# Attention on pairs of heads: alternating row halves and column halves of the array

## The chip, the cores and the metric

The kernel runs on one core of one Trainium2 chip. The metric is the device time of one execution in microseconds (us). "The span" is the time from the first to the last instruction of the profiled execution. The engines are named as the profile names them: PE is TensorE (matmuls and transposes), PEld its weight loads, DVE is VectorE, ACT is ScalarE, POOL is GpSimd, SP issues the DMAs.

## The reference

The program is one decoder block on 256 tokens and 1024 features: two attention branches, gated and mixed, and then a layer of 16384 experts. What matters here is the attention, 8 heads of 64 features in both branches, over two blocks of 128 query tokens. `o_cmp` attends to 15 compressed tokens; with 256 tokens all four selection blocks are chosen, and the window of 512 covers everything, so `o_sel` and `o_win` are plain causal attention with different keys and values.

```python
def block_fn(bidx):
    ...
    sc = jnp.einsum('bghtd,bgcd->bghtc', qb, kc) * scale
    pc = jax.nn.softmax(jnp.where(cmask, sc, NEG), axis=-1) * has_c
    o_cmp = jnp.einsum('bghtc,bgcd->bghtd', pc, vc)
    ...
    ps = jax.nn.softmax(jnp.where(smask[:, :, None], ss, NEG), axis=(-2, -1))
    o_sel = jnp.einsum('bghtnl,bgtnld->bghtd', ps, vs_g)
    ...
    pw = jax.nn.softmax(jnp.where(wmask, sw, NEG), axis=-1)
    o_win = jnp.einsum('bghtk,bgkd->bghtd', pw, vwb)
    o_nsa = gb[0] * o_cmp + gb[1] * o_sel + gb[2] * o_win
    z = jnp.einsum('bhtd,bhsd->bhts', qsb, k_sb) * scale
    m = pos[None, :] < t[:, None]
    l1m = jnp.where(m, jax.nn.log_sigmoid(-z), 0.0)
    after = lax.cumsum(l1m, axis=3, reverse=True) - l1m
    a_w = jnp.where(m, jnp.exp(jax.nn.log_sigmoid(z) + after), 0.0)
    o_sb = jnp.einsum('bhts,bhsd->bhtd', a_w, v_sb)
```

## The kernel before

The order of every engine is written out by hand, and semaphores tie the engines together. Everything up to the experts is a stream of 78 weight tiles of 128x1024 floats. SP loads tile n into `raw[n % 4]`; ACT copies it to `hi[n % 3]` in the reduced type fp32r (`split_hi(n)`, L749), DVE writes the rest to `lo[n % 3]` (`split_lo(n)`, L1094), and PE multiplies by both. So `split_hi(n)` must wait until PE has used tile n-3. A tile of the gates (`gate_tile(g)`, tile `T_GATE + g`, g from 0 to 15) is 24 matmuls of 128x256 into PSUM bank `g % 2`; ACT reads it with `gate_exp(g)` (L870).

The eight heads lie between the last tile of `vsb` (L344 to L346) and the mixing of the branches (`branch(0)`, first line L575). In the loop over heads `hh` PE does, in this order:

- `gate_tile(2 * hh)`;
- six transposes of the probabilities of this head (L519) and two of its compressed ones (L523); called T below;
- `scores(hh + 1)`: the score products of the next head (L471, L472, L474); called S;
- the sums of logs of the stick branch, with triangular and all-ones weights (L531 to L533); called L;
- `gate_tile(2 * hh + 1)`;
- `sticks(hh + 1)`: the stick products (L486, L487);
- the value products (L546 to L548 for the first branch, L553 and L554 for the stick branch); called V.

All these products are in f32, and PE executes each as two instructions, so a row of the profile with x2 is one product. The scores and sticks contract over the 64 features of a head. Those of an even head lie on partitions 0 to 63 and those of an odd head on 64 to 127, so only half of the array's rows takes part. The value products give 64 output partitions, 0 to 63 for an even head and 64 to 127 for an odd one, so only half of its columns takes part.

```python
r0, a, g = 64 * (hh % 2), hh // 2, hh // 4
r = slice(r0, r0 + HD)
```

Around PE the chain of a head is this. The softmax: DVE adds the mask (L1268, L1269) and takes maxima (L1274 to L1277), ACT exponentiates in six pieces with their sums (`exps`, L879), DVE normalises (L1292 to L1296), PE transposes, ACT copies the transposes out (L903). The sticks: ACT takes Abs, Exp and Ln (`softplus`, L864 to L866), DVE makes two arrays from it (`stick_logs`, L1284, L1285), POOL masks one (L1575), PE sums, DVE adds (`x_ready`, L1314), ACT exponentiates (L907), POOL masks again (L1580), PE multiplies by the values, ACT copies both results out (`osb_out`, L887). Before the loop ACT copies the stick values out of banks 2 and 1 (`vsb_out`, L894, L895).

Of the kernel before, what the change touches and what calls it, by code (L numbers as in the profile page):

```python
# [30 lines left out]
P = 128  # L31
# [57 lines left out]
def build(nc, x_d, wpre_d, u_d, v_d, par_d, cst_d, kep_d, out_d):  # L89
    with ExitStack() as ctx:  # L90
# [66 lines left out]
        gcc, gsc = carve(64), carve(64)  # L157
        nrm_n, nrm_a, nrm_b, nrm_q, nrm_c = carve(512), carve(512), carve(512), carve(512), carve(128)
# [16 lines left out]
        sm = carve(2 * 828).rearrange("p (q c) -> p q c", q=2)  # L175
        att = carve(2 * 32).rearrange("p (q c) -> p q c", q=2)
        pT = carve(1024)
        sbt = carve(5 * 384).rearrange("p (k c) -> p k c", k=5)
# [136 lines left out]
        def _(pe):  # L315
# [145 lines left out]
            def scores(hh):  # L461
                r0, a, g = 64 * (hh % 2), hh // 2, hh // 4
                r = slice(r0, r0 + HD)
                if hh == 0:
                    pe.wait_ge(S("qkT_out"), 4)
                    pe.wait_ge(S("kcT_out"), 1)
                else:
                    pe.wait_ge(S("masked"), hh)
                for br, o in ((0, bank[4]), (1, bank[5])):
                    k = kT[r, 2 * br + g, :]  # L470
                    pe.matmul(o[:, 0:P], qT[r, a, 0:P], k[:, 0:P], start=True, stop=True)  # L471
                    m = pe.matmul(o[:, P:384], qT[r, a, P:T], k[:, 0:T], start=True, stop=True)  # L472
                for b in range(TB):
                    m = pe.matmul(bank[4][:, 384 + NC_ * b:384 + NC_ * (b + 1)], qT[r, a, b * P:(b + 1) * P],  # L474
                                  kcT[r, g, 0:NC_], start=True, stop=True)
                m.then_inc(S("scores"), 1)

            def sticks(hh):
                r0, a = 64 * (hh % 2), hh // 2
                r = slice(r0, r0 + HD)  # L480
                if hh == 0:
                    pe.wait_ge(S("qksb_out"), 4)
                    pe.wait_ge(S("vsb_out"), 1)
                else:
                    pe.wait_ge(S("x_ready"), hh)
                pe.matmul(bank[2][:, 0:T], ksbT[r, a, 0:P], qsbT[r, a, :], start=True, stop=True)  # L486
                m = pe.matmul(bank[2][:, T:384], ksbT[r, a, P:T], qsbT[r, a, P:T], start=True, stop=True)  # L487
# [12 lines left out]
            for i in range(4):  # L500
                normal(T_VSB + i, i, [bank[2][:, :], bank[1][:, :]])
                if i == 0:
                    scores(0)
            sticks(0)
            for hh in range(NH):
                r0, a, g = 64 * (hh % 2), hh // 2, hh // 4
                gate_tile(2 * hh)

                pe.wait_ge(S("probs"), hh + 1)
                if hh == 0:  # L510
                    pe.wait_ge(S("qksb_out"), 4)
                else:
                    pe.wait_ge(S("pT_out"), 2 * hh)
                    pe.wait_ge(S("cmpT_out"), hh)
                    pe.wait_ge(S("osb_out"), hh)
                q = hh % 2
                for br in range(2):
                    for c in range(3):
                        m = pe.transpose(bank[6 + br][:, c * P:(c + 1) * P],  # L519
                                         sm[:, q, 414 * br + c * P:414 * br + (c + 1) * P], ident)  # L520
                m.then_inc(S("pT"), 1)
                for b in range(TB):
                    m = pe.transpose(bank[3][0:NC_, b * P:(b + 1) * P],  # L523
                                     sm[:, q, 384 + NC_ * b:384 + NC_ * (b + 1)], ident)
                m.then_inc(S("cmpT"), 1)
                if hh + 1 < NH:
                    scores(hh + 1)

                pe.wait_ge(S("l_masked"), hh + 1)
                L = sbt[:, 1, :]  # L530
                pe.matmul(bank[2][:, 0:T], cv_("tri"), L[:, 0:T], start=True, stop=False)  # L531
                pe.matmul(bank[2][:, P:T], cv_("ones"), L[:, T:384], start=False, stop=True)
                m = pe.matmul(bank[2][:, T:384], cv_("tri"), L[:, T:384], start=True, stop=True)  # L533
                m.then_inc(S("after"), 1)
                if hh + 1 < NH:
                    gate_tile(2 * hh + 1)
                    sticks(hh + 1)

                pe.wait_ge(S("pT_out"), 2 * hh + 2)
                pe.wait_ge(S("cmpT_out"), hh + 1)  # L540
                o = bank[3][r0:r0 + HD, 0:T]
                for br in range(2):
                    vcol = slice((2 * br + g) * HD, (2 * br + g + 1) * HD)
                    p0 = 384 * br

                    pe.matmul(o, vsw[:, 0, vcol], pT[:, p0:p0 + T], start=(br == 0), stop=False)  # L546
                    pe.matmul(o[:, P:T], vsw[:, 1, vcol], pT[:, p0 + T:p0 + 384], start=False, stop=False)
                m = pe.matmul(o, vcs[0:NC_, g * HD:(g + 1) * HD], pT[0:NC_, 768:1024], start=False, stop=True)  # L548
                m.then_inc(S("onsa"), 1)
                pe.wait_ge(S("a_ready"), hh + 1)  # L550
                o = bank[3][r0:r0 + HD, T:2 * T]
                vcol = slice(hh * HD, (hh + 1) * HD)
                pe.matmul(o, vsb[:, 0, vcol], sbt[:, 4, 0:T], start=True, stop=False)  # L553
                m = pe.matmul(o[:, P:T], vsb[:, 1, vcol], sbt[:, 4, T:384], start=False, stop=True)  # L554
                m.then_inc(S("osb"), 1)

# [179 lines left out]
        def _(act):  # L736
# [121 lines left out]
            def softplus(hh):  # L858

                act.wait_ge(S("z_ready"), hh + 1)  # L860
                if hh:
                    act.wait_ge(S("z_read"), hh)
                sp_ = sbt[:, 2, :]
                link(act.activation(sp_, bank[2][:, 0:384], ACT.Abs))  # L864
                link(act.activation(sp_, sp_, ACT.Exp, scale=-1.0))
                act.activation(sp_, sp_, ACT.Ln, bias=1.0).then_inc(S("softplus"), 1)  # L866

            def gate_exp(g):
                act.wait_ge(tile_used, T_GATE + g + 1)
                act.activation(gates[:, g, :], bank[g % 2][:, 0:T], ACT.Exp,  # L870
                               scale=-1.0).then_inc(S("gate_exp"), 1)

            def exps(hh):

                q = hh % 2
                act.wait_ge(S("negmax"), hh + 1)
                for c, (c0, w_) in enumerate(((0, P), (P, T), (414, P), (414 + P, T), (384, NC_), (384 + NC_, NC_))):
                    x_ = sm[:, q, c0:c0 + w_]
                    m = act.activation(x_, x_, ACT.Exp, bias=att[:, q, 6 + c:7 + c], scale=SCALE,  # L879
                                       accum_out=att[:, q, 12 + c:13 + c])  # L880
                m.then_inc(S("exped"), 1)

            def osb_out(hh):

                r0, a = 64 * (hh % 2), hh // 2
                act.wait_ge(S("osb"), hh + 1)
                act.activation(oT.rearrange("p (k a) t -> p k a t", k=2)[r0:r0 + HD, :, a, :],  # L887
                               bank[3][r0:r0 + HD, :].rearrange("p (k t) -> p k t", k=2), ACT.Copy).then_inc(S("osb_out"), 1)

            exps(0)  # L890
            split_hi(31)
            split_hi(32)
# [3 lines left out]
            softplus(0)  # L896
            for hh in range(NH):
                split_hi(T_GATE + 2 * hh + 3)
                act.wait_ge(S("pT"), hh + 1)
                if hh:  # L900
                    act.wait_ge(S("onsa"), hh)
                for br in range(2):
                    act.activation(pT[:, 384 * br:384 * (br + 1)], bank[6 + br][:, 0:384],  # L903
                                   ACT.Copy).then_inc(S("pT_out"), 1)
                gate_exp(2 * hh)
                act.wait_ge(S("x_ready"), hh + 1)
                act.activation(sbt[:, 0, :], sbt[:, 0, :], ACT.Exp).then_inc(S("x_exp"), 1)  # L907
                if hh + 1 < NH:
                    exps(hh + 1)
                    osb_out(hh)  # L910
                    softplus(hh + 1)
# [861 lines left out]
```

## Time and profile before

| what | value |
|---|---|
| time, median of 3 runs (lowest to highest) | 1107.07 us (1105.69 to 1108.93) |
| the profiled execution: its time | 1109.66 us |
| the profiled execution: its span, mean granted clock | 1107.9 us, 0.995 |
| PE busy | 1081.7 us, 98% of the span |
| DVE busy | 876.1 us, 79% |
| ACT busy | 695.8 us, 63% |
| the heads: end of the first `vsb` tile to the start of `branch(0)` | 92.95 to 216.87 us |

A busy PE is not a full PE: matmuls are pipelined, so the time that one costs in a sequence is the distance from its start to the start of the next, not its own duration.

### The profile page before, as it was taken

What the parts mean: (1) busy time and instruction counts of PE and PEld (TensorE: products, weight loads), DVE (VectorE), ACT (ScalarE), POOL (GpSimd) and SP (SyncE); (2) the same over time, 40 slices, a digit from 0 to 9 for tenths busy, and PEclk for the clock granted to TensorE, in tenths of its full rate; (3) what the DMA queues carried; (4) which work ended last, traced back from release to release, by engine and by line L of the source; (5) the groups of instructions that cost most, each with busy time, mean ns of one, the idle gap of its engine ahead of it and who ended that gap; (6) DMA issues with size and microseconds to landing.
All of it is one profiled execution on the core that took longest, in us unless ns stands there. A gap on an engine that the chain in (4) does not pass through costs nothing.

```text
span 1107.9 us, 22321 instructions
## 1 busy us (share of the span) xinstructions
PE 1081.7 (98%) x7162; PEld 979.0 (88%) x7162; DVE 876.1 (79%) x1702; ACT 695.8 (63%) x1246; POOL 331.8 (30%) x286
## 2 busy tenths in 40 slices
PE   6999999999999999999999999999999999999998
PEld 5788888798999999999999999978888888888887
DVE  5754666577999998988999999999999996444444
ACT  4345665566444444447777777799999996554443
POOL 0000122100700111662333333224444444445553
PEclk9999999899999999999999999999999999999999
DMA  7464122255545556554444444444444455555553
GB/s 258 148 234 153 58 77 78 75 189 162 202 135 178 183 171 199 180 184 145 166 151 163 159 153 164 158 152 165 160 169 162 160 175 204 190 195 195 196 190 114
DMA packets 50017, 181.34 MB, mean 164 GB/s; under 512 B 5552, under 2 KB 5680, under 8 KB 49968
## 3 DMA queue, kind: packets, MB, share of 16 engines
q1 hardware_dynamic: 49968, 180.72, 48.3%
q8 instruction: 27, 0.44, 0.2%
q14 instruction: 22, 0.18, 0.1%
HBM read 178.60 MB, written 2.10 MB: 163 GB/s over the span
## 4 chain that ended last, share of the span: by engine, by line
PE 89%; DVE 7%; ACT 2%; DMA 1%; issue 1%; POOL 0%; SPq 0%; ACTq 0%; POOLq 0%; DVEq 0%
PE bank L713 32%; PE bank L658 10%; PE bank L659 9%; PE bank L660 9%; PE bank L672 5%; PE bank L330 4%; PE bank L331 4%; PE bank L332 3%; DVE lo L1376 2%; PE bank L599 2%; DMA raw<-wpre_d 1%; PE bank L344 1%; PE bank L345 1%; PE bank L346 1%; PE bank L546 1%; PE bank L408 1%
## 5 line engine op out<-in xcount | busy, mean ns | idle before, releaser
L970 ACT ACTIVATE hi<-raw 128x1024 fp32r<-128x1024 f32 x253 | 268.2, 1061 | 245.8 <-PE bank L660 151.3
L1376 DVE TENSOR_TENSOR lo<-raw,hi 128x1024 fp32r<-128x1024 f32 x253 | 315.3, 1251 | 104.7 <-ACT hi L970 103.9
L658 PE MATMUL bank<-xhi,hi 128*128 128x256 f32 x1024 | 293.6, 287 | 0.8 <-DVE lo L1376 0.8
L659 PE MATMUL bank<-xlo,hi 128*128 128x256 f32 x1024 | 289.5, 283 | 0.0
L660 PE MATMUL bank<-xhi,lo 128*128 128x256 f32 x1024 | 289.4, 283 | 0.0
L1635 POOL TENSOR_TENSOR auxl<-big,auxh 128x256 fp32r<-128x256 f32 x126 | 168.9, 1341 | 200.2 <-ACT auxh L1006 200.2
L658 PEld LDWEIGHTS bank<-xhi,hi 128*128 128x128 f32 x1024 | 196.0, 191 | 2.2 <-issue 1.2
L659 PEld LDWEIGHTS bank<-xlo,hi 128*128 128x128 f32 x1024 | 196.3, 192 | 0.0
L660 PEld LDWEIGHTS bank<-xhi,lo 128*128 128x128 f32 x1024 | 196.0, 191 | 0.0
L713 PE MATMUL bank<-hi,auxh 128*128 128x512 f32 x508 | 161.2, 399 | 0.5 <-POOL auxl L1635 0.3
L713 PE MATMUL bank<-lo,auxh 128*128 128x512 f32 x508 | 157.2, 391 | 0.0
L713 PE MATMUL bank<-hi,auxl 128*128 128x512 f32 x508 | 156.8, 390 | 0.0
L1094 DVE TENSOR_TENSOR lo<-raw,hi 128x1024 fp32r<-128x1024 f32 x73 | 96.5, 1331 | 43.5 <-ACT hi L749 43.1
L749 ACT ACTIVATE hi<-raw 128x1024 fp32r<-128x1024 f32 x73 | 76.9, 1056 | 63.2 <-PE bank L332 39.6
L713 PEld LDWEIGHTS bank<-lo,auxh 128*128 128x128 f32 x508 | 95.3, 188 | 21.1
L713 PEld LDWEIGHTS bank<-hi,auxl 128*128 128x128 f32 x508 | 95.4, 188 | 20.7
L1622 POOL TENSOR_TENSOR oneB<-kep,eT 128x512 fp32r<-128x512 f32 x64 | 66.9, 1047 | 150.3 <-PE bank L672 140.5
L713 PEld LDWEIGHTS bank<-hi,auxh 128*128 128x128 f32 x508 | 90.6, 189 | 16.6 <-POOL auxl L1635 0.8
L1506 DVE TENSOR_REDUCE gsum<-bank 128x256 f32<-128x512 f32 x128 | 87.6, 685 | 7.7 <-PE bank L672 1.5
L1497 DVE TENSOR_TENSOR oneA<-same,gw 128x512 fp32r<-128x512 f32 x128 | 87.2, 681 | 0.0
L1000 ACT ACTIVATE oneB<-oneB 128x512 fp32r<-128x512 f32 x128 | 80.1, 626 | 2.1
L993 ACT ACTIVATE oneB<-kep,eT 128x128 fp32r<-128x128 f32 x256 | 81.0, 388 | 0.0
(270 smaller groups left out, 1773.6 us busy)
## 6 DMA issues: line engine op xcount, KB each, us to landing
raw<-u_d SPq DMA_DIRECT2D x128, 512.0 KB, 3.3
raw<-v_d SPq DMA_DIRECT2D x128, 512.0 KB, 3.2
raw<-wpre_d SPq DMA_DIRECT2D x78, 512.0 KB, 4.0
big<-x_d SPq DMA_DIRECT2D x2, 512.0 KB, 3.7
out_d<-big SPq DMA_DIRECT2D x2, 512.0 KB, 5.5
big<-out_d SPq DMA_DIRECT2D x2, 512.0 KB, 5.1
out_d<-big SPq DMA_DIRECT2D x4, 256.0 KB, 2.1
big<-cst_d SPq DMA_DIRECT2D x1, 719.5 KB, 8.1
```

The lines of the kernel that those rows point to most:

```text
L658: pe.matmul(out, wh, xhi[:, k, :], start=(k == 0), stop=False)
L659: pe.matmul(out, wh, xlo[:, k, :], start=False, stop=False)
L660: m = pe.matmul(out, wl, xhi[:, k, :], start=False, stop=(k == KT - 1))
L713: m = pe.matmul(bank[2 * b + f][:, :], a_, w_[:, s, f * 512:(f + 1) * 512], start=(first and st_ == 0), stop=False, skip_group_check=True)
L970: act.activation(hi[:, n % SPLIT, :], raw[:, n % RING, :], ACT.Copy).then_inc(hi_done, 1)
L993: m = act.activation(oneB[:, g % 2, t, :], iota, ACT.Square, bias=i2, scale=-1.0)
L1000: act.activation(oneB[:, g % 2, :, :], oneB[:, g % 2, :, :].bitcast(F32), ACT.Relu, bias=1.0, scale=-1.0).then_inc(S("oneB_ready"), 1)
L1094: dve.tensor_tensor(lo[:, n % SPLIT, :], raw[:, n % RING, :], hi[:, n % SPLIT, :].bitcast(F32), ALU.subtract).then_inc(lo_done, 1)
L1376: dve.tensor_tensor(lo[:, n % SPLIT, :], raw[:, n % RING, :], hi[:, n % SPLIT, :].bitcast(F32), ALU.subtract).then_inc(lo_done, 1)
L1497: dve.tensor_tensor(oneA[:, g % 2, :, :, :], eq_, w_.unsqueeze(3).broadcast_to([P, 4, 2, HALF]), ALU.mult).then_inc(S("oneA_ready"), 1)
L1506: dve.tensor_reduce(gsum[:, :, :], parts, AXX, ALU.add).then_inc(S("bank67_read"), 1)
L1635: pool.tensor_tensor(auxl[:, s * T:(s + 1) * T], big[:, bass.ds(i * (UNROLL * T) + b * T, T)], auxh[:, s * T:(s + 1) * T].bitcast(F32), AL ...
```

## The change

Four pairs `p` take the place of eight heads. Within `scores`, `sticks` and the value products the calls of the two heads of a pair stand in turn: one on the lower half of the rows (or columns), the next on the upper half. The score products of the two heads go to banks 4 and 5, the sticks to banks 2 and 1, both value results to bank 3 on the two halves of its partitions. The gate tiles lose bank 1 and all use bank 0, so each waits for the `gate_exp` of the one before. ACT, DVE and POOL do the same work on the same elements; what can be done for two heads in one instruction is (Exp, Ln, the maxima, the masks of the sticks, the copy of the results). The scores come in two steps per pair, one per branch, each waiting for DVE to have read the one before.

```diff
+            rows = (slice(0, HD), slice(HD, P))
+            def scores(p, br):
...
+                    pe.wait_ge(S("masked"), 2 * p + br)
+                for c0, q_, w_ in ((0, slice(0, P), P), (P, slice(P, T), T)):
+                    for i, r in enumerate(rows):
+                        m = pe.matmul(bank[4 + i][:, c0:c0 + w_], qT[r, p, q_], kT[r, 2 * br + g, 0:w_],
+                                      start=True, stop=True)
+                if br == 0:
+                    for b in range(TB):
+                        for i, r in enumerate(rows):
+                            m = pe.matmul(bank[4 + i][:, 384 + NC_ * b:384 + NC_ * (b + 1)], qT[r, p, b * P:(b + 1) * P],
+                                          kcT[r, g, 0:NC_], start=True, stop=True)
...
             def gate_tile(g):
-                if g >= 2:
-                    pe.wait_ge(S("gate_exp"), g - 1)
+                if g:
+                    pe.wait_ge(S("gate_exp"), g)
                 else:
-                    pe.wait_ge(S("vsb_out"), 2)
-                tposed(T_GATE + g, bank[g % 2][:, 0:T])
+                    pe.wait_ge(S("kcT_out"), 1)
+                tposed(T_GATE + g, bank[0][:, 0:T])
...
+                for br in range(2):
+                    vcol = slice((2 * br + g) * HD, (2 * br + g + 1) * HD)
+                    p0 = 384 * br
+                    for i, r in enumerate(rows):
+                        pe.matmul(bank[3][r, 0:T], vsw[:, 0, vcol], pT[i][:, p0:p0 + T], start=(br == 0), stop=False)
+                    for i, r in enumerate(rows):
+                        pe.matmul(bank[3][r, P:T], vsw[:, 1, vcol], pT[i][:, p0 + T:p0 + 384], start=False, stop=False)
...
+            for p in range(4):
+                gate_tile(4 * p)
+                if p == 0:
+                    sticks(0)
+                probs_T(p, 0)
+                gate_tile(4 * p + 1)
+                probs_T(p, 1)
+                if p < 3:
+                    scores(p + 1, 0)
+                if p:
+                    log_sums(p)
+                gate_tile(4 * p + 2)
+                if p == 0:
+                    log_sums(p)
+                if p < 3:
+                    scores(p + 1, 1)
+                    sticks(p + 1)
+                    gate_tile(4 * p + 3)
+                by_values(p)
             gate_tile(2 * NH - 1)
...
+            for p in range(4):
+                gate_exp(4 * p)
+                if p == 0:
+                    softplus(0)
+                pT_out(p, 0)
+                split_hi(T_GATE + 4 * p + 3)
+                gate_exp(4 * p + 1)
+                split_hi(T_GATE + 4 * p + 4)
+                pT_out(p, 1)
+                act.wait_ge(S("x_ready"), p + 1)
+                act.activation(stick_x, stick_x, ACT.Exp).then_inc(S("x_exp"), 1)
+                gate_exp(4 * p + 2)
+                split_hi(T_GATE + 4 * p + 5)
+                if p < 3:
+                    softplus(p + 1)
+                    gate_exp(4 * p + 3)
+                    exps(p + 1, 0)
+                    osb_out(p)
+                    exps(p + 1, 1)
+                    split_hi(T_GATE + 4 * p + 6)
+            osb_out(3)
...
+            for p in range(4):
+                split_lo(T_GATE + 4 * p + 3)
+                split_lo(T_GATE + 4 * p + 4)
...
+                split_lo(T_GATE + 4 * p + 5)
+                if p < 3:
+                    mask_scores(p + 1, 1)
+                    maxima(p + 1)
+                    stick_logs(p + 1)
+                    normalise(p + 1, 0)
+                    normalise(p + 1, 1)
+                    split_lo(T_GATE + 4 * p + 6)
```

The first place is PE's scores and sums of logs, inside the loop. Before, one head's scores are followed by its sums (L471 to L474 are the scores, L531 to L533 the sums):

```order
L471 MATMUL bank<-big 128x128
L472 MATMUL bank<-big 128x256
L471 MATMUL bank<-big 128x128
L472 MATMUL bank<-big 128x256
L474 MATMUL bank<-big 128x15 x2
L531 MATMUL bank<-big 128x256
L532 MATMUL bank<-big 128x128
L533 MATMUL bank<-big 128x128
```

In the change the four calls of a row such as `128x256 x2` or `128x15 x4` belong to both heads in turn, and the first branch's scores of a pair stand ahead of the sums of the pair before, the second branch's behind the next gate tile:

```order
L479 MATMUL bank<-big 128x128 x2
L479 MATMUL bank<-big 128x256 x2
L484 MATMUL bank<-big 128x15 x4
L532 MATMUL bank<-big 128x256
L533 MATMUL bank<-big 128x128
L534 MATMUL bank<-big 128x128
L532 MATMUL bank<-big 128x256
L533 MATMUL bank<-big 128x128
L534 MATMUL bank<-big 128x128
```

What moved: the same products for two heads stand together, in one run for the first branch and one for the second, instead of in one run for each head.

The second place is PE's value products. Before, for one head (L546 to L548 into partitions of the first branch's result, L553 and L554 for the sticks):

```order
L546 MATMUL bank<-big 64x256
L547 MATMUL bank<-big 64x128
L546 MATMUL bank<-big 64x256
L547 MATMUL bank<-big 64x128
L548 MATMUL bank<-big 64x256
L553 MATMUL bank<-big 64x256
L554 MATMUL bank<-big 64x128
```

In the change, for a pair:

```order
L546 MATMUL bank<-big 64x256 x2
L548 MATMUL bank<-big 64x128 x2
L546 MATMUL bank<-big 64x256 x2
L548 MATMUL bank<-big 64x128 x2
L550 MATMUL bank<-big 64x256 x2
L556 MATMUL bank<-big 64x256 x2
L559 MATMUL bank<-big 64x128 x2
```

Each call now has its twin on the other column half right behind it.

The third place is ACT at the end of an iteration. Before (L879 is `exps`, L887 `osb_out`, L864 to L866 `softplus`, L749 `split_hi`, L870 `gate_exp`):

```order
L879 ACTIVATE big<-big 128x15 x2
L887 ACTIVATE big<-bank 64x2x256
L864 ACTIVATE big<-bank 128x384
L865 ACTIVATE big<-big 128x384
L866 ACTIVATE big<-big 128x384
L749 ACTIVATE hi<-raw 128x1024
L870 ACTIVATE big<-bank 128x256
```

In the change (L909 is `exps`, L925 `osb_out`, L780 `split_hi`, L901 `gate_exp`):

```order
L909 ACTIVATE big<-big 128x256
L909 ACTIVATE big<-big 128x15 x2
L925 ACTIVATE big<-bank 128x2x256
L909 ACTIVATE big<-big 128x128
L909 ACTIVATE big<-big 128x256
L909 ACTIVATE big<-big 128x128
L909 ACTIVATE big<-big 128x256
L909 ACTIVATE big<-big 128x15 x2
L780 ACTIVATE hi<-raw 128x1024
L901 ACTIVATE big<-bank 128x256
```

Two runs of `exps` with `osb_out` between them and one `split_hi` now stand ahead of the `gate_exp` that the second gate tile of the next pair waits for.

## Rows read from the trace of the kernel before

**Rows 1.** The page: busy time by engine; the group of `split_lo`.

```profile
PE 1081.7 (98%) x7162; PEld 979.0 (88%) x7162; DVE 876.1 (79%) x1702; ACT 695.8 (63%) x1246; POOL 331.8 (30%) x286
...
L1094 DVE TENSOR_TENSOR lo<-raw,hi 128x1024 fp32r<-128x1024 f32 x73 | 96.5, 1331 | 43.5 <-ACT hi L749 43.1
```

**Rows 2.** Stretches: length, busy time of PE, PEld, DVE, ACT, POOL, granted clock.

```profile
208.00:217.00 9.00, 9.00 (x40) 6.52 (x41) 1.52 (x2) 2.18 (x3) 0.99 (x1) 0.62 0.20 72
...
123.70:137.10 13.40, 13.40 (x94) 11.44 (x93) 8.65 (x21) 8.04 (x24) 2.95 (x2) 1.00 0.25 80
```

**Rows 3.** PE in time: start, duration, line, shape (weights' rows*columns, moving operand).

```profile
110.30 0.82 PE L519 MATMUL bank<-kep,big 128*128 128x128 f32 x6
...
111.27 0.49 PE L471 MATMUL bank<-big 64*128 64x128 f32 x2
111.59 0.59 PE L472 MATMUL bank<-big 64*128 64x256 f32 x2
112.03 0.38 PE L471 MATMUL bank<-big 64*128 64x128 f32 x2
...
112.68 0.51 PE L474 MATMUL bank<-big 64*128 64x15 f32 x4
113.12 0.70 PE L531 MATMUL bank<-big 128*128 128x256 f32 x2
...
114.03 0.36 PE L330 MATMUL bank<-xhi,hi 128*128 128x256 f32 x1
...
117.06 0.70 PE L486 MATMUL bank<-big 64*128 64x256 f32 x2
...
117.91 0.65 PE L546 MATMUL bank<-big 128*64 128x256 f32 x2
118.39 0.38 PE L547 MATMUL bank<-big 128*64 128x128 f32 x2
118.61 0.60 PE L546 MATMUL bank<-big 128*64 128x256 f32 x2
...
120.73 0.38 PE L330 MATMUL bank<-xhi,hi 128*128 128x256 f32 x1
```

**Rows 4.** PE in time where it waits: before the loop and in its last head.

```profile
105.05 0.67 PE L486 MATMUL bank<-big 64*128 64x256 f32 x2 [1.78 <-ACT big L894]
...
206.48 0.70 PE L531 MATMUL bank<-big 128*128 128x256 f32 x2 [1.30 <-POOL big L1575]
...
207.98 0.87 PE L546 MATMUL bank<-big 128*64 128x256 f32 x2 [0.36 <-DVE big L1310]
...
216.87 0.28 PE L575 MATMUL bank<-oneB,hi 128*128 128x256 f32 x1
```

**Rows 5.** DVE in time, one head.

```profile
127.84 0.54 DVE L1269 TENSOR_TENSOR big<-bank,big 128x384 f32<-128x384 f32 x1
128.41 0.42 DVE L1274 TENSOR_REDUCE big<-big 128x2 f32<-128x256 f32 x1
128.75 0.68 DVE L1275 TENSOR_REDUCE big<-big 128x2 f32<-128x512 f32 x1
...
133.53 1.29 DVE L1296 TENSOR_SCALAR big<-big 128x128 f32<-128x128 f32 x6
```

**Rows 6.** ACT in time, the next head.

```profile
144.18 0.39 ACT L879 ACTIVATE big<-big 128x128 f32<-128x128 f32 x1
...
147.65 0.60 ACT L887 ACTIVATE big<-bank 64x512 f32<-64x512 f32 x1 [1.04 <-PE bank L554]
...
149.64 1.04 ACT L749 ACTIVATE hi<-raw 128x1024 fp32r<-128x1024 f32 x1
150.59 0.36 ACT L870 ACTIVATE big<-bank 128x256 f32<-128x256 f32 x1
```

**Rows 7.** Groups between 110.2 and 204 us: count, busy us, mean ns, idle before.

```profile
L1575 POOL TENSOR_TENSOR big<-big 128x384 f32<-128x384 f32 x6 | 11.6, 1940 | 34.7 <-DVE big L1285 34.7
...
L1580 POOL TENSOR_TENSOR big<-big 128x384 f32<-128x384 f32 x7 | 7.1, 1010 | 35.8 <-ACT big L907 35.8
```

More of the change, by code:

```diff
@@ L157, in build @@
         gcc, gsc = carve(64), carve(64)
+        nrm_at = at[0]
         nrm_n, nrm_a, nrm_b, nrm_q, nrm_c = carve(512), carve(512), carve(512), carve(512), carve(128)
@@ L467, in scores @@
                 else:
[L468 to L475, printed above, removed]
+                    pe.wait_ge(S("masked"), 2 * p + br)
@@ new lines, in log_sums @@
+            def log_sums(p):
+                pe.wait_ge(S("l_masked"), p + 1)
+                for i in range(2):
+                    L = stick_l[:, i, :]
+                    pe.matmul(z_bank[i][:, 0:T], cv_("tri"), L[:, 0:T], start=True, stop=False)
+                    pe.matmul(z_bank[i][:, P:T], cv_("ones"), L[:, T:384], start=False, stop=True)
+                    m = pe.matmul(z_bank[i][:, T:384], cv_("tri"), L[:, T:384], start=True, stop=True)
+                m.then_inc(S("after"), 1)
@@ L501, in _ @@
                 normal(T_VSB + i, i, [bank[2][:, :], bank[1][:, :]])
[L502 to L555, printed above, removed]
@@ L856, in _, with softplus @@
                 split_hi(n)
[L858 to L866, printed above, removed]
+            def softplus(p):
+                act.wait_ge(S("z_ready"), p + 1)
+                if p:
+                    act.wait_ge(S("z_read"), p)
+                for i in range(2):
+                    link(act.activation(stick_p[:, i, :], z_bank[i][:, 0:384], ACT.Abs))
+                link(act.activation(stick_p, stick_p, ACT.Exp, scale=-1.0))
+                act.activation(stick_p, stick_p, ACT.Ln, bias=1.0).then_inc(S("softplus"), 1)
@@ L881, in exps, with pT_out @@
                 m.then_inc(S("exped"), 1)
[L883 to L890, printed above, removed]
+            def pT_out(p, i):
+                act.wait_ge(S("pT"), 2 * p + i + 1)
+                if p:
+                    act.wait_ge(S("onsa"), p)
+                for br in range(2):
+                    act.activation(pT[i][:, 384 * br:384 * (br + 1)], bank[6 + br][:, 0:384],
+                                   ACT.Copy).then_inc(S("pT_out"), 1)
@@ L891, in _, with osb_out @@
+            def osb_out(p):
+                act.wait_ge(S("osb"), p + 1)
+                act.activation(oT.rearrange("p (k a) t -> p k a t", k=2)[:, :, p, :],
+                               bank[3][:, :].rearrange("p (k t) -> p k t", k=2), ACT.Copy).then_inc(S("osb_out"), 1)
+            exps(0, 0)
             split_hi(31)
-            split_hi(32)
+            exps(0, 1)
             act.wait_ge(tile_used, T_VSB + 4)
@@ L895, in _ @@
             act.activation(vsb[:, 1, :], bank[1][:, :], ACT.Copy).then_inc(S("vsb_out"), 1)
[L896 to L911, printed above, removed]
-                    split_hi(T_GATE + 2 * hh + 4)
-                    gate_exp(2 * hh + 1)
-            osb_out(NH - 1)
-            act.wait_ge(S("osb_out"), NH)
+            split_hi(32)
+            for p in range(4):
+                gate_exp(4 * p)
+                if p == 0:
+                    softplus(0)
[16 more added lines that the diff above has]
+            osb_out(3)
+            act.wait_ge(S("osb_out"), NH // 2)
             act.activation(ohi[0], oT[:, 0:4, :], ACT.Copy).then_inc(S("oT_hi"), 1)
```

200 lines of the change are left out of this document (123 added, 77 removed).

## The prediction

> **What bounds the kernel now.** I read the page first: PE is busy 98% of the span [rows 1], so the question is which stretch of PE the change touches and whether anything else would stop PE there. The table of stretches shows one head of the loop, 13.4 us long: PE busy for all of it, DVE 8.65 us, ACT 8.04 us, POOL 2.95 us [rows 2]. PE's timeline then gives the cost of each step as the distance between starts [rows 3]: T 0.97 us (110.30 to 111.27), S 1.85 (to 113.12), L 0.91 (to 114.03), gate tile 3.03 (to 117.06), sticks 0.85 (to 117.91), V 2.82 (to 120.73). With the second gate tile, about 3.0, a head is 13.4 us, and nothing in it is a wait. So every us that PE saves here is a us of the kernel, until one of the chains through ACT and DVE is late. PE does wait at the two ends [rows 4]: 1.78 us for ACT's copies of the stick values before the loop, and 1.30 and 0.36 us in the last head. After those last waits the granted clock falls to 0.62 in the stretch from 208 to 217 us [rows 2], a mean over the two levels, 1.2 and 2.4 GHz. From 207.98 to 216.87 PE does V and one gate tile in 8.89 us, where at full clock they take 2.82 + 3.03 = 5.85: 3.04 us lost.
>
> **The unit costs inside these steps** [rows 3]. A product with 256 columns moving takes 0.44 us (111.59 to 112.03), one with 128 columns 0.22 (118.39 to 118.61). The four instructions with only 15 columns take 0.44 us (112.68 to 113.12), 0.11 each, the same as an instruction with 128 columns. So there is a floor of 0.11 us for an instruction that loads 128 columns of weights, however little it multiplies. The first product behind the transposes takes 0.32 (111.27 to 111.59) where its like takes 0.22: 0.10 us to go from the full array to half of it.
>
> **What overlap would give.** No row of before shows two instructions on different halves at once, since each head stays on one half. The bounds come from the unit costs. If the halves work side by side, two 256-column products take 0.44 instead of 0.88. For two 128-column products the saving lies between 0.22 (all side by side) and nothing (the floor of 0.11 per instruction stays, because the weight loads still go one behind the other). The 15-column ones lie between 0.44 saved per pair and nothing. I take the floor for the rows' halves, where the 15-column row is the nearest evidence, and the middle for the value products, whose weights have only 64 columns. For a pair of heads:
>
> - S: before 3.70. Now 2 x 0.44 (256) + 2 x 0.44 (128, at the floor) + 0.88 (eight 15-column instructions at 0.11) + 0.2 (entering the half array twice) = 2.84.
> - Sticks: before 1.70. Now 0.44 + 0.44 + 0.1 = 0.98.
> - V: before 5.64. Now four 256-column pairs 1.76, three 128-column pairs between 0.66 and 1.32, and about 0.35 for entries and exits (the 15-row product among them): 2.8 to 3.4, taken as 3.1.
> - Gate tiles, T and L are the same instructions: 12.0 + 1.94 + 1.82.
>
> Saved per pair: 0.86 + 0.72 + 2.54 = 4.1 us, so **16.5 us** over four pairs. With everything side by side it would be 5.5 per pair, 22 us.
>
> For the sums above the row of 15 columns decides for the floor. The Trainium skill ("TensorEngine Tiling (Array Packing)", Key Properties) says that different tiles can load weights and multiply in parallel, which would put the saving at the upper bound, 22 us; no row of before can show it.
>
> **What the new order makes PE wait for.** The second gate tile of a pair now waits for the first one's `gate_exp`, because bank 1 went to the sticks. On ACT that `gate_exp` stands behind two `exps`, `osb_out` and a `split_hi`. And `exps` can't begin before DVE has the maxima of both branches, which stand behind the `split_lo` of tile 4p+5, whose `split_hi` waits until PE has used gate tile 4p+2. I follow that chain from the end of gate tile 4p+2, each piece as distance between starts or the duration less the 0.1 us by which neighbours overlap:
>
> - ACT `gate_exp` 0.3, `split_hi` 0.95 [rows 6], DVE `split_lo` 1.25 (mean 1.33, a mean that holds some stretched by POOL [rows 1]), two mask additions 2 x 0.57, maxima over twice the elements: 0.42 for 256 and 0.68 for 512 elements [rows 5] make 0.58 + 1.1, and 0.4 for the small ones; hand-offs 0.4. Sum 6.1 us.
> - ACT: one `exps` is 2.43 (144.18 to 146.61, where the idle 1.04 before 147.65 begins), `osb_out` 0.5, again 2.43, `split_hi` 0.95, `gate_exp` 0.3 [rows 6], hand-offs 0.3. Sum 6.9, together 13.0 us.
> - PE meanwhile: S of the second branch 0.98, sticks 0.98, gate tile 3.0, V 3.1, gate tile 3.0, T 0.97: 12.0 us.
>
> So PE waits about **1.0 us** in a transition from pair to pair. The transposes ahead of it come in time: the normalised probabilities are there at 6.1 + 2.43 + 1.7 (1.29 for the six multiplications and 0.4 ahead of them [rows 5]) + 0.2 = 10.4 us, and PE wants them at 11.1. The first transition is longer: in pair 0 L stands behind gate tile 2, so everything hangs on the end of L: x_ready 1.3, Exp over 768 elements 0.85, then as above from `gate_exp` on, 15.0 us against 12.1 of PE: 2.9. The last pair has no successor. Waits added: 2.9 + 2 x 1.0 = **4.9 us**. Queued behind DVE's waiting `split_lo` are exactly the masks, maxima and `stick_logs` named here; behind ACT's, `softplus`. Both are in the sum. The cover ends at 6 us after the gate tile: with a PE 2 us faster the wait is 2 us longer, so saving beyond my value is worth half to nothing.
>
> **The ends.** Before the loop, the first gate tile no longer waits for ACT's copies; the first sticks, behind it, do. Those copies come some 3.9 us later (one more `exps`, 2.43, and maxima that need the second branch's scores behind the second `vsb` tile). PE comes 4.0 us later (gate tile 3.0, twice the scores 0.98). The 1.78 us of wait stay, with +0.4 taken for it, and so does the low clock behind it. In the last pair V waits for POOL's second mask: x_ready 1.3, Exp 0.85, POOL 2 x 1.01 [rows 7], hand-offs 0.3, 4.5 us behind L; gate tile and the first part of V cover 5. If POOL's multiplication is stretched as L1575 was (1.94 [rows 7]) 1.4 us of wait show. L has its input early there. So I take away the 1.66 us of waits and the 3.04 us of low clock: **4.7 us**.
>
> ACT, DVE and POOL do the same elements in fewer instructions. Their loads for a pair, about 17, 16 and 6 us, fit into 22.7 + 1.0. SP's loads run further ahead of PE than one gate tile and are costed at nothing; without that cover a tile's load would appear as a wait of its `split_hi`.
>
> **Sum:** -16.5 + 4.9 + 0.4 - 4.7 = -15.9 us. Against the profiled execution: 1109.66 (span 1107.9 and 1.8 around it) becomes 1093.8. That execution lies 2.6 above the median of the runs, and I carry the difference over to the median: 1107.07 - 15.9 = **1091 us**. With everything side by side: -22 + 7.0 (waits 1.7, 1.7, 3.6) + 0.4 - 4.7 = -19.3, 1088.
>
> **Rivals.**
>
> - *Only the row halves overlap.* For it: V is a different case, one set of rows feeding two moving operands, and nothing in the rows shows it. V then saves only its entries and exits, 0.3. Saved 4 x 1.9 = 7.6, waits 1.5: -7.6 + 1.5 + 0.4 - 4.7 = -10.4, **1097 us**. Here a rule speaks: the Trainium skill ("TensorE: Matmul & The Clock Gate", The mechanism) has a weight load overlap running matmuls only when the row group differs, which the two column halves don't fulfil; the same page's table nevertheless gives three column tiles 2.38 times the speed.
> - *No overlap: the change doesn't do what it says.* The f32 products are two instructions each, and the second of one head stands between the first of both; if PE takes them strictly one by one, S, sticks and V save some 0.5 per pair. -2 + 1.5 + 0.4 - 4.7 = -4.8, **1102 us**, all of it from the quiet end. If the last pair waits after all, this is a tie.
> - *The chains are longer.* POOL's masks over 768 elements now lie beside `normalise` and `split_lo`, and L1094 and L1575 stretched each other before (means 1331 and 1940 ns [rows 1, 7]). 1 to 2 us more in each of three transitions: **1094 to 1098 us**.
> - *Slower: each change of half drains the array.* Entering the half array cost 0.10 us. If each step from one half to the other costs that too, a pair has 12 + 4 + 14 = 30 of them: 4 x 3.0 = 12 us on top of the case without overlap, **1114 us**. It decides for slower from 0.04 us per step on (4.8 / 120). Against it: the halves are one arrangement of the array, and the row shows a cost only for changing the arrangement.
>
> **How the numbers follow.** Halves overlap both ways (1086 to 1094): 0.50. Chains longer: 0.12. Rows only: 0.12. No overlap: 0.15. A cost for each step: 0.07. Something else: 0.04. The range reaches from the upper bound of the overlap with a little less waiting, 1084, to the case without overlap, 1103. A difference of 0.3%, 3.3 us, is about what a measurement of this kernel can tell from none. Faster: the first three cases and two thirds of the fourth, 0.83. Within 0.3%: 0.08. Slower: 0.09.
>
> **What the profile after would show.** Right: the score instructions of both heads start within 0.02 us of each other in twos, S of a first branch about 1.85 us, of a second 0.98, V near 3.1; PE's longest waits in the loop in front of the second gate tile of a pair, for ACT's `gate_exp`; granted clock 1.00 in the last pair. Wrong: starts evenly 0.22 us apart (no overlap), or a gap with every change of half; V at 5.3 (rows only); the waits in front of the transposes (DVE late) or of L (POOL late), more than 2 us each. What would make it wrong as a whole is a low clock through the loop, set off by waits that come every 23 us.

## The result and the profile after

The changed kernel takes 1087.38 us, median of 4 runs (1086.62 to 1088.09), against 1106.51 us (4 runs) before: ratio 0.983, 95% interval 0.9815 to 0.984, 18 to 20 us faster. Five runs on another occasion gave 1086.51 us against 1107.22 us, ratio 0.9815 (0.980 to 0.983). The profiled execution took 1086.62 us, with a span of 1084.8 us. The page, busy time by engine:

```profile
PE 1057.9 (98%) x7162; PEld 961.7 (89%) x7162; DVE 873.5 (81%) x1686; ACT 691.7 (64%) x1230; POOL 324.9 (30%) x278
```

Stretches of the changed kernel, with the columns of [rows 2]:

```profile
107.20:112.00 4.80, 4.79 (x42) 4.65 (x43) 2.91 (x8) 4.71 (x9) 0.00 (x0) 1.00 0.57 200
...
127.10:137.75 10.65, 8.63 (x59) 7.94 (x58) 8.30 (x22) 8.10 (x30) 1.85 (x1) 0.84 0.13 43
...
190.80:196.00 5.20, 4.87 (x40) 4.41 (x36) 2.08 (x2) 3.61 (x5) 0.00 (x0) 1.00 0.27 101
137.75:160.10 22.35, 21.62 (x187) 19.05 (x185) 16.50 (x36) 15.51 (x42) 3.69 (x2) 1.00 0.24 77
```

From a second table of stretches of the same execution:

```profile
133.00:138.00 5.00, 4.92 (x30) 4.45 (x28) 3.38 (x8) 2.25 (x6) 0.00 (x0) 0.67 0.32 106
```

The last line of the first table is one whole pair, from its second T to the same place in the next pair: 22.35 us, where two heads took 26.8. PE is busy 21.62 us of it. PE in time over that pair:

```profile
137.75 0.82 PE L519 MATMUL bank<-kep,big 128*128 128x128 f32 x6
...
138.71 0.93 PE L479 MATMUL bank<-big 64*128 64x128 f32 x8
139.48 0.51 PE L484 MATMUL bank<-big 64*128 64x15 f32 x8
139.92 0.70 PE L532 MATMUL bank<-big 128*128 128x256 f32 x2
...
144.74 0.93 PE L479 MATMUL bank<-big 64*128 64x128 f32 x8
145.50 0.60 PE L495 MATMUL bank<-big 64*128 64x256 f32 x4
145.93 0.39 PE L497 MATMUL bank<-big 64*128 64x128 f32 x4
...
149.31 0.65 PE L546 MATMUL bank<-big 128*64 128x256 f32 x4
...
150.02 0.60 PE L546 MATMUL bank<-big 128*64 128x256 f32 x4
...
150.77 0.65 PE L550 MATMUL bank<-big 15*64 15x256 f32 x4
151.35 0.65 PE L556 MATMUL bank<-big 128*64 128x256 f32 x4
151.84 0.39 PE L559 MATMUL bank<-big 128*64 128x128 f32 x4
...
155.75 0.88 PE L519 MATMUL bank<-kep,big 128*128 128x128 f32 x6 [0.46 <-DVE big L1345]
...
160.10 0.82 PE L519 MATMUL bank<-kep,big 128*128 128x128 f32 x6
```

Here x8 and x4 are four and two products. In the row at 144.74 the first instructions of the two heads both start at 144.74, the sign that the prediction named. The scores of a first branch, four products with 128 and 256 columns and four with 15, take from 138.71 to 139.92: 1.21 us. The eight 15-column instructions take 0.44 us (139.48 to 139.92), as long as four did before. The second branch takes 0.76 us (144.74 to 145.50). Together that is 1.97 us for two heads, where one took 1.85 [rows 3]. The values of two heads take 1.46 (149.31 to 150.77) + 0.58 + 0.49 + 0.31: 2.84 us, what one head took before. PE's waits from 88 to 212 us (line waited for, us in total, times, longest):

```profile
PE bank L519 <- DVE big L1345: 2.9, 3, 1.9
...
PE bank L495 <- ACT big L933: 1.6, 1, 1.6
...
PE bank L336 <- ACT big L901: 0.8, 3, 0.3
```

The three waits in front of the transposes are 1.94, 0.46 and 0.46 us. There is one more, of 0.25 us in front of the second pair's sticks (L1370, at 120.05). The first wait of the transposes ends at 132.18, and behind it the granted clock is low: a mean of 0.67 from 133 to 138 us, and 0.84 in the longer stretch from 127.10 to 137.75. At the end of the last pair, 190.8 to 196, it is 1.00 where it was 0.62 before [rows 2]. PE waits for DVE's normalising, and that holds something that was not in the sum. DVE (first fence) and POOL (second) in the same 3 us:

```profile
153.07 0.19 DVE L1341 RECIPROCAL big<-big 128x6 f32<-128x6 f32 x1 [0.66 <-ACT big L909]
153.29 1.08 DVE L1342 TENSOR_TENSOR big<-big 128x6 f32<-128x6 f32 x1
154.40 1.29 DVE L1345 TENSOR_SCALAR big<-big 128x128 f32<-128x128 f32 x6
...
156.11 0.17 DVE L1342 TENSOR_TENSOR big<-big 128x6 f32<-128x6 f32 x1
```

```profile
152.49 1.86 POOL L1637 TENSOR_TENSOR big<-big 128x768 f32<-128x768 f32 x1 [6.60 <-DVE big L1334]
```

The small multiplication L1342 over 128x6 numbers takes 1.08 us at 153.29 and 0.17 us at 156.11. The first lies beside POOL's mask over 768 elements, which ends at 154.35, just where the multiplication does.

### The profile page after: what moved, and what is told of

It reads as the page before. It is cut to its first block, busy times and chain, and to the rows that moved or that the text cites. A ratio compares the mean times of both kernels' runs of the same rounds, so it can differ in the third digit from the quotient of the medians.

```text
span 1084.8 us, 22245 instructions
## 1 busy us (share of the span) xinstructions
PE 1057.9 (98%) x7162; PEld 961.7 (89%) x7162; DVE 873.5 (81%) x1686; ACT 691.7 (64%) x1230; POOL 324.9 (30%) x278
## 4 chain that ended last, share of the span: by engine, by line
PE 85%; DVE 8%; ACT 4%; DMA 1%; issue 1%; POOL 0%; SPq 0%; ACTq 0%; POOLq 0%; DVEq 0%
PE bank L744 32%; PE bank L689 10%; PE bank L690 9%; PE bank L691 9%; PE bank L703 5%; PE bank L336 3%; PE bank L337 3%; PE bank L338 3%; DVE lo L1437 2%; PE bank L630 2%; ACT big L909 2%; DMA raw<-wpre_d 1%; ACT hi L780 1%; PE bank L350 1%; PE bank L352 1%; PE bank L351 1%
## 5 line engine op out<-in xcount | busy, mean ns | idle before, releaser
L780 ACT ACTIVATE hi<-raw 128x1024 fp32r<-128x1024 f32 x73 | 76.8, 1056 | 58.8 <-PE bank L338 36.6
```

The costliest lines, as they stand in the source:

```text
L780: act.activation(hi[:, n % SPLIT, :], raw[:, n % RING, :], ACT.Copy).then_inc(hi_done, 1)
```

## The experiments

For all kernels I read one length besides the time: from the first scores before the loop to the first instruction of `branch(0)`. The time of a run holds what comes ahead of it too, and the first scores start anywhere from 91.3 to 95.3 us in the profiles below; the length repeats within 0.15 us in the two kernels that were profiled twice (102.12 and 101.99 in two profiles of the changed kernel, 97.51 and 97.49 in two of the masks-first kernel). Before has one profile, of an execution 2.6 us above its median, so its length is somewhat longer than a typical one.

| kernel | median us | ratio to before (95%) | length us |
|---|---|---|---|
| before | 1106.51 | 1 | 123.92 |
| changed | 1087.38 | 0.983 (0.9815 to 0.984) | 102.12 |
| head by head | 1091.57 | 0.987 (0.984 to 0.989) | 106.34 |
| rows only | 1090.56 | 0.986 (0.984 to 0.988) | 105.67 |
| columns only | 1087.40 | 0.983 (0.981 to 0.985) | 101.35 |
| scores and sticks on the same half | 1092.71 | 0.987 (0.985 to 0.989) | 109.35 |
| all on one half | 1103.00 | 0.9975 (0.996 to 0.999) | 116.76 |
| values head by head, short ones last | 1087.27 | 0.983 (0.981 to 0.9845) | 101.77 |
| masks first | 1082.95 | 0.979 (0.9775 to 0.981) | 97.51 |
| masks and normalise | 1082.35 | 0.9785 (0.977 to 0.980) | 97.52 |
| copies first | 1082.48 | 0.9775 (0.976 to 0.979) | 97.47 |

**Is it the neighbourhood of the twins?** Head by head: the loops over the heads of a pair go outside.

```diff
-                for c0, q_, w_ in ((0, slice(0, P), P), (P, slice(P, T), T)):
-                    for i, r in enumerate(rows):
+                for i, r in enumerate(rows):
+                    for c0, q_, w_ in ((0, slice(0, P), P), (P, slice(P, T), T)):
```

The same is done for the 15-column products, the sticks and the values.

> The changed kernel with its pairs, banks and queue orders, but within scores, sticks and value products all calls of the even head stand ahead of all calls of the odd head, so twins no longer stand side by side. Theory A (the halves of the array work at the same time when twins are adjacent): the scores of a first branch take about 2.3 us instead of 1.20, of a second 1.4 instead of 0.86, sticks 1.4 instead of 0.75, values 5.2 instead of 2.84; 4.7 us per pair, 19 us in all, less about 3.5 us of waits that this covers: about 1103 us, ratio to before near 0.996. Theory B (the gain comes from the new order, fewer entries into half the array and the quiet last pair): within 3 us of the changed kernel, 1087 to 1090 us.

The length grew by 4.2 us, not by 15. Neither theory had it. PE in time:

```profile
137.50 0.93 PE L479 MATMUL bank<-big 64*128 64x128 f32 x8
138.26 0.62 PE L484 MATMUL bank<-big 64*128 64x15 f32 x8
...
148.31 0.65 PE L545 MATMUL bank<-big 128*64 128x256 f32 x2
...
149.76 0.64 PE L547 MATMUL bank<-big 15*64 15x256 f32 x2
150.33 0.65 PE L545 MATMUL bank<-big 128*64 128x256 f32 x2
...
151.78 0.64 PE L547 MATMUL bank<-big 15*64 15x256 f32 x2
152.36 0.66 PE L553 MATMUL bank<-big 128*64 128x256 f32 x4
```

The scores still take 0.76 us (137.50 to 138.26), as with alternating twins, and the stick values (152.36 on) are as short as well. The eight 15-column instructions take 0.55 us (138.26 to 138.81) instead of 0.44. Only the first branch's values went from 2.04 to 4.05 us (148.31 to 152.36), head behind head. So the halves overlap without being written in turn, but not everywhere. The two partial kernels are in line with that: rows only carries the values' loss, columns only a small one.

> The changed kernel with only the value products head by head; scores and sticks still alternate. Theory A (both kinds of halves overlap): values go from 2.84 to about 5.2 us per pair, 9.4 us in all, less 3 to 4 us of waits in front of the transposes that this covers: 1092 to 1094 us. Rival (only row halves overlap, the columns gained from something else): no change, 1087 us.

Measured 1090.56 us, 3.2 above the changed kernel: the column halves do overlap there, since taking the turns away costs time. On PE the cost is 2.0 us per pair, 8.0 in all, and it is the cover that makes it look small: this kernel has no wait in front of the transposes (2.9 us in the changed kernel), and its clock stays at 1.00 from 104 to 200 us, so the low clock of about 1.5 us is gone too. The time came out below the expected range, because the stick values kept their overlap and the expectation did not count the low clock.

> The changed kernel with scores and sticks head by head; the value products still alternate. Theory A: scores and sticks of a pair go from 2.8 to about 5.1 us, 9.2 us in all, less 1 to 3 us of waits: 1094 to 1096 us. If the gain were only in the order: 1087 us.

Measured 1087.40, no difference in the time. The expectation was wrong; adjacent twins are not needed for four products. A small cost there is: the 15-column products take 0.1 us more per pair, and the second branch's scores with the sticks 1.6 us instead of 1.5, so about 0.8 us in four pairs. It doesn't show because this kernel did not have the low clock behind 132 us; its length is even 0.8 us shorter.

**Are different halves needed?** The odd head's rows are replaced by the even head's in scores and sticks:

```diff
+            low = (slice(0, HD), slice(0, HD))
-                    for i, r in enumerate(rows):
+                    for i, r in enumerate(low):
```

> Part of the computation is changed: for scores and sticks the odd head of a pair is computed with the even head's features, so both calls use the lower row half; they still alternate between two banks. The value products stay. Theory A (overlap needs different halves of the rows): like the kernel with only the columns alternating, 1094 to 1096 us, scores of a first branch near 2.3 us. Rival (alternating between two banks, or batching like shapes, is enough): 1087 us, scores 1.20 us.

PE in time, this kernel:

```profile
143.17 1.57 PE L480 MATMUL bank<-big 64*128 64x128 f32 x8
144.58 0.95 PE L485 MATMUL bank<-big 64*128 64x15 f32 x8
145.47 0.70 PE L533 MATMUL bank<-big 128*128 128x256 f32 x2
```

The four large products of the scores took 1.41 us instead of 0.76, the 15-column ones 0.89 instead of 0.44. The same calls, order and banks, only on one half of the rows: the overlap is gone. Different halves are what it takes. The time is 1092.71 us, below the 1094 to 1096 expected; the wait in front of the transposes went from 2.9 to 1.4 us.

**How much of the gain is overlap?**

> Part of the computation is changed: for scores, sticks and value products the odd head of each pair uses the even head's rows and writes to the even head's partitions, and the value products stand head by head, so no two products can use different halves of the array. Everything else is the changed kernel. Theory A (overlap of the halves is worth most of the gain): the stages of a pair take 2.3 + 1.4 + 1.3 + 5.0 us instead of 1.2 + 0.8 + 0.75 + 2.8, some 4.5 us per pair, 18 in all, less 3 to 4 us of waits that go under: 1100 to 1103 us, so 13 to 16 of the 19 us are overlap and the rest is order and the quiet end. Theory B (order and the last pair are worth most): under 1095 us.

PE in time, the kernel with all on one half:

```profile
143.63 1.57 PE L480 MATMUL bank<-big 64*128 64x128 f32 x8
145.05 0.96 PE L485 MATMUL bank<-big 64*128 64x15 f32 x8
145.93 0.70 PE L533 MATMUL bank<-big 128*128 128x256 f32 x2
...
150.75 1.57 PE L480 MATMUL bank<-big 64*128 64x128 f32 x8
152.17 1.02 PE L496 MATMUL bank<-big 64*128 64x256 f32 x4
153.03 0.60 PE L498 MATMUL bank<-big 64*128 64x128 f32 x4
```

First-branch scores take 2.30 us (143.63 to 145.93), second-branch ones 1.42, the 256-column sticks 0.86 (152.17 to 153.03) instead of 0.43: two heads one behind the other. The time is 1103.00 us. So of the 19 us, about 15.6 are overlap, net of the waits and the low clock that came with it, and the rest is 3.3 us; its ratio to before, 0.996 to 0.999, allows 0.7 to 4.9 for that rest. In the length it is 14.6 of 21.8. The two are not quite parted: head by head, this kernel also enters and leaves the 15-row product twice per pair where the changed kernel does it once.

**What keeps the two heads' values apart?** In the head-by-head order a 15-row product stands between the heads. Here it is moved behind both:

```diff
                 for i, r in enumerate(rows):
                     for br in range(2):
...
+                for i, r in enumerate(rows):
+                    m = pe.matmul(bank[3][r, 0:T], vcs[0:NC_, g * HD:(g + 1) * HD], pT[i][0:NC_, 768:1024],
+                                  start=False, stop=True)
```

> Value products head by head as in the rows-only kernel, but with the two 15-row products (15 rows of weights, another arrangement of the array) moved behind the eight full-height ones. In the head-by-head kernels the scores and the stick values overlapped although twins stood apart, and only the first branch's value products, with a 15-row product between the heads, did not. Theory C (the change of arrangement at the 15-row product is what keeps the two heads apart; distance alone doesn't): the ten products take 2.0 to 2.4 us instead of 4.0, and the time is within 1 us of the changed kernel's, 1087 to 1088.5. Theory D (PE looks ahead only over a few instructions; eight are too many): they take about 3.5 to 4.0 us and the time is 1090 to 1091.

PE in time, this kernel; L546 has 256 columns, L547 128, and each head has both twice:

```profile
148.79 0.65 PE L546 MATMUL bank<-big 128*64 128x256 f32 x2
149.28 0.38 PE L547 MATMUL bank<-big 128*64 128x128 f32 x2
149.50 0.65 PE L546 MATMUL bank<-big 128*64 128x256 f32 x4
149.93 0.44 PE L547 MATMUL bank<-big 128*64 128x128 f32 x4
150.21 0.60 PE L546 MATMUL bank<-big 128*64 128x256 f32 x2
150.64 0.38 PE L547 MATMUL bank<-big 128*64 128x128 f32 x2
150.96 0.65 PE L549 MATMUL bank<-big 15*64 15x256 f32 x4
```

Eight products take 2.17 us (148.79 to 150.96); alternating they take 1.46, and one head behind the other twice 1.45 (148.31 to 149.76 in the head-by-head kernel). So the overlap came back in part, and both theories have a piece: with the 15-row products all ten take 2.74 us (to 151.53), between the 2.4 of C and the 3.5 of D. The time, 1087.27 us, is as C had it, but only because less waiting covers the 0.7 us per pair: 1.3 instead of 2.9 us in front of the transposes, and no low clock. The row x4 at 149.50 is the even head's third product together with the odd head's first. A closer look, instructions running at 150.1 us:

```profile
149.77 0.38 PE L546 MATMUL bank<-big 128*64 128x256 f32 x1
149.93 0.44 PE L547 MATMUL bank<-big 128*64 128x128 f32 x4
```

The last of the four L546 instructions, which are the even head's third product and the odd head's first, starts at 149.77; the even head's fourth product, which stands ahead of the odd head's first in the program, starts at 149.93. Here PE starts a product on the idle half two products ahead of its turn: not when the even head's first or second product starts, but with its third. In the scores of the head-by-head kernel two is all it takes. Whether what limits it is counted in products, in instructions or in time, no run shows. With the 15-row product between the heads, the odd head's first product would also have been two behind the even head's fourth, and nothing overlapped. So the change of arrangement acts as a barrier; that it is the 15 rows and nothing else about this product was not tried on another one. The Trainium skill says that changing the tiling mode drains the array ("TensorEngine Tiling (Array Packing)", Key Properties), and these rows agree if 15 rows count as another mode than 128. Two other rules of the Trainium skill don't hold here ("TensorE: Matmul & The Clock Gate", The mechanism). One is that matmuls start strictly in program order, against 149.77 before 149.93. The other is that weight loads overlap running matmuls only when the row group differs: the value products of two heads use the same rows and different columns, and they take 2.84 us where one after the other would take 5.6.

**Where do the remaining waits come from?** On DVE, `split_lo(T_GATE + 4 * p + 5)` goes behind `mask_scores(p + 1, 1)` and `maxima(p + 1)`:

```diff
-                split_lo(T_GATE + 4 * p + 5)
                 if p < 3:
                     mask_scores(p + 1, 1)
                     maxima(p + 1)
+                split_lo(T_GATE + 4 * p + 5)
```

> The changed kernel with one move on DVE: the split of tile 4p+5 stands behind the second branch's mask additions and the maxima, instead of ahead of them. If the waits of the changed kernel in front of the transposes (1.94, 0.46, 0.46 us) are the end of the chain split, masks, maxima, exponentials, normalising, all three nearly vanish, and with the first of them the low clock behind it (about 1.6 us): 1083 to 1084.5 us. Rival (POOL holding up DVE's small multiplication, 1.07 us instead of 0.17, is what makes them): that stays, the waits shrink by less than half, 1086 to 1087 us.

> As the masks-first kernel, and the first head's normalising stands ahead of the two stick arrays on DVE, so that POOL's mask no longer lies beside it. If the masks alone remove the waits: the same as that kernel within 0.5 us, 1083 to 1084.5. If POOL is what matters: 1083 to 1084.5 only here, and the other at 1086 to 1087.

1082.95 and 1082.35 us, lengths 97.51 and 97.52. PE's waits in the masks-first kernel, apart from the same 0.25 us in front of the second pair's sticks:

```profile
PE bank L495 <- ACT big L933: 1.6, 1, 1.6
...
PE bank L336 <- ACT big L901: 0.5, 2, 0.3
```

The waits in front of the transposes are gone, and the clock is granted in full from 104 us on. 4.6 us less in the length: 2.9 of waits in front of the transposes, 0.3 in front of gate tiles, the rest low clock behind the first wait. DVE's small multiplication still takes 1.07 to 1.47 us beside POOL there, and it costs nothing any more; moving it away from the first head only moved it to the second (1.8 us), without a change. So the order on DVE is enough by itself. Whether keeping POOL's mask away from the multiplication, in the old order, would have been enough too was not tried: by the numbers it would be for the two waits of 0.46 us (0.9 us of stretch), and not for the one of 1.94. Both kernels are faster than the changed one.

Last, the wait in front of the first sticks, on top of the masks-first order: ACT's two `vsb_out` copies go ahead of `exps(0, 1)`.

> The masks-first kernel, and ACT copies the stick values out of banks 2 and 1 ahead of the second head's exponentials before the loop, so that PE no longer waits 1.6 us in front of the first sticks. Theory E (the 1.6 us are on the path): 1.3 to 1.6 us less than the masks-first kernel, 1081.5. Theory F (the first sums of logs hang on the chain sticks, softplus, stick arrays, POOL, and the second gate tile on an exponential that now comes after 2.4 us of others, so that the wait only moves there): 0 to 0.7 us less, 1082.3 to 1083, and a wait of about 1 us in front of a gate tile instead.

> The masks-first kernel once more, beside the copies-first kernel on the same chip, as its reference: 1082 to 1084 us.

> The changed kernel once more, beside these two on the same chip: 1087 to 1088 us, 4 to 5 us above the masks-first kernel.

1082.48, 1083.51 and 1086.51 us; the first two can't be told apart, and their lengths are 97.47 and 97.49. The changed kernel is 3.0 us above the masks-first one here, not 4 to 5 as expected, and 4.5 in the length (101.99). PE in time, copies first:

```profile
107.02 0.70 PE L495 MATMUL bank<-big 64*128 64x256 f32 x4
...
109.81 0.38 PE L336 MATMUL bank<-xhi,hi 128*128 128x256 f32 x1 [0.83 <-ACT big L901]
...
113.31 0.85 PE L519 MATMUL bank<-kep,big 128*128 128x128 f32 x6 [0.38 <-ACT big L919]
```

The sticks at 107.02 wait no longer, and the next gate tile and the next transposes wait 0.83 and 0.38 us for ACT instead. Most of what this kernel spares at one place comes back at the next (1.2 of 1.6 us), as theory F had it. Gate tiles on two halves of bank 0, so that they don't wait for `gate_exp`, were not tried.

## Why the prediction was right

Forecast 1091 us, range 1084 to 1103; measured 1087.4. The likeliest case came in, and its mechanism is shown: with all products on one half the kernel takes 1103.0 us, close to the 1102 worked out for no overlap. That the number is so close is in part luck. For the profiled execution the forecast was 1093.8 us and it took 1086.6, 7.2 less. The overlap was forecast too small, and the gain at the ends was read from an execution of before with more low clock than most: it took 1109.66 us at a mean granted clock of 0.995, while another one, at 1.00, took 1103.93.

- **The overlap** was mis-sized. I kept a floor of 0.11 us per instruction for the weight loads of the two heads and took the middle for the values. There is no such floor between halves: eight 15-column instructions take what four did, first-branch scores 1.21 us (I had about 1.85), values 2.84 (3.1). Saved per pair: 26.8 - 21.6 = 5.2 us, 21 in all, against 16.5 forecast and 22 as the upper bound.
- **The added waits** were 4.0 us (2.9 in front of transposes, 0.8 in front of gate tiles, 0.3 in front of sticks), forecast 4.9, or 7.0 for full overlap. The chain I followed was the right one, as the masks-first kernel shows, and its first part measured 5.8 us from the end of gate tile 4p+2 to the maxima (144.74 to 150.5) against 6.1. But I had PE's longest wait in front of the second gate tile; it was in front of the transposes. The probabilities were there 11.0 us behind the gate tile (155.75) instead of 10.4, because `normalise` took 0.9 us more beside POOL, and PE wanted them at 10.5 instead of 11.1. And I had not counted a low clock behind the first wait: 1.5 us (132.18 to 137.75 is 5.57; the same steps a pair later, 155.75 to 160.10, take 4.35, and 0.27 of that is a wait for a gate tile that the first transition doesn't have).
- **The start.** The wait of 1.78 us stayed, as 1.59. The low clock behind it, which I carried over, did not come: before, the first gate tile took 4.4 us (105.86 to 110.30 [rows 3]), now everything from 107.2 to 112 runs at 1.00. That is 1.4 us more gained. It is not owed to the change for certain: in the kernel with scores and sticks on the same half, the same wait of 1.6 us was followed by a clock of 0.81 from 108 to 113 us.
- **The quiet end** came as forecast: no wait in the last pair, clock 1.00. 4.7 us.
- **Together:** -20.8 + 4.0 + 1.5 - 0.2 - 1.4 - 4.7 = -21.6, and the length shrank by 21.8 us. The medians give 19 to 21. The profiled execution of before was 2.6 us above its median, so the profiles' spans differ by more (23.1) than the times do.
- **The rivals.** Rows only and no overlap: refuted by the rows-only kernel and by the two with products moved to the same half. A cost for each change of half: the rows at 138.71 have none. Longer chains: the POOL part is there (1.08 instead of 0.17 us), 0.9 us in each transition.

## What to carry to other kernels

Where a product uses half of the array's rows or of its columns, put one for the other half within two products of it, with no product of another shape of array between them. Strict alternation was not needed for most of the gain, but it overlapped best here: head by head cost 0.2 us per pair in scores and sticks, 0.7 in the four first-branch values, and 2.0 with the 15-row product between. A faster PE brings the next chain to light: follow it from the step that releases it, and look on each engine for work ahead of it in the queue that nobody waits for yet. One `split_lo` moved on DVE was worth another 3 to 4.5 us. And a cost that waits cover (8.0 us of values on PE, 3.2 in the time) is not a small cost: it shows once the waits are gone. A wait at one place is only worth what the next one leaves of it.

## What was not expected of the hardware

Two f32 products overlap as completely as the rows can tell, weight loads included, for row halves and for column halves, and in the one order that shows it PE starts one two products ahead of its turn. A wait of PE of the same length may or may not be followed by a low clock. Behind 1.6 us in front of the first sticks it stayed at its upper level (2.4 GHz) in the changed kernel and fell to a mean of 0.81 in the one with scores and sticks on the same half; behind 1.94 us in front of the transposes it fell in the changed kernel (mean 0.67 from 133 to 138 us), and behind 2.0 us at the same place it stayed at 1.00 in the columns-only kernel, whose length is 0.8 us shorter. What decides between them, these runs don't tell. DVE's 128x6 multiplication of 0.17 us takes up to 1.8 us while POOL multiplies 128x768.
